# Three stretches of a hybrid decoder layer in another order: state-space outputs by kind, the attention projection's weights piece by piece, and the output projection's first weight splits among the mixed tiles

## The chip, the cores and the metric

The kernel runs on one core of a Trainium2 chip. The metric is the device time of one execution in microseconds (us). Engines are named as in the profile: PE is TensorE (PEld its weight loads), DVE VectorE, ACT ScalarE, POOL GpSimd, SP SyncE, which here only issues transfers. A q behind an engine's name (SPq) is its instruction queue.

## What is computed

One layer of a decoder trunk for 512 prompt tokens and 32 sample tokens (8 sequences of 4), all float32, model width 1024. Cut to what matters here:

```
h = x + 1/2 SwiGLU(RMSNorm(x));  n = RMSNorm(h);  P = n @ w_in
    [u | q | k | v | q_idx | k_idx | w_idx | gate_s5 | gate_att] = columns of P
S5  = GLU(GELU(y)),  s_t = A s_(t-1) + B u_t,  y = Re(C s_t) + D u_t   # 32 groups of 16 channels, 64 states
DSA = softmax attention over the top-k keys of an indexer, @ w_att_proj (512 x 1024)
h = h + (sigmoid(gate_s5) * S5 + sigmoid(gate_att) * DSA) @ w_out      # w_out 1024 x 1024
h = h + 1/2 SwiGLU(RMSNorm(h));  y = RMSNorm(h)
```

Outputs are y, the new keys, values and index keys, and the last states, for prompt and sample.

## The kernel before

Each engine runs an instruction stream written by hand; semaphores (`wait_ge`, `then_inc`) are all that ties them together. Nothing is scheduled by a planner, so the order in the code is the order on each engine. The 544 tokens are the moving columns of the large products, in two halves of 272 (`HALF`); weights are stationary in tiles of 128 x 128. The order is: first FFN, input projection, state-space part with the index scores, a loop of 32 steps for the prompt's attention, the sample's attention over the paged cache, attention projection, output projection, second FFN, final norm.

**State-space outputs** (PE, L833). `outputs(q4)` handles four pairs of groups; there are four calls, so 16 pairs in all. For one pair `gp` it writes columns `c0` to `c0+128` of two PSUM banks with three kinds of product: the lag kernels (`toep`, 128 rows by 72 columns of the array, L839), the carried states (`vst` against `yre` and `yim`, 64 rows by 64 columns, L842) and the sample's first states (`s0`, 64 rows by 8 columns, L847). The last two come in pairs, one on rows 0 to 63 and one on rows 64 to 127. The trace has two records for each float32 product. ACT copies the banks out (L1322), PE turns them (L855), and ACT applies GELU. ACT then issues eight transfers (L1349) that read a table of distance biases from DRAM into `biasmem`, where `yre` and `yim` lay. The sample's index scores follow on PE. POOL issues the first page of cached keys (L425) once these scores are done, and then waits for the bias table before it adds it to the masks (L1578) for the attention loop. In that loop PE's scores (L955) are taken over by DVE (L1893), and PE's next scores wait for that.

**Attention projection** (PE, L1083 to L1090). Before it the sample's values are gathered: eight steps of products with pages (L1065) run for each of two rounds, and each frees a page buffer and raises `kv_used` by one. `page_load` reuses four page buffers in turn. The weights `attw[0..3]` (512 KB each, L530, on SP's queue) lie where pages lay: `attw[0]` in pages of buffer 0, `attw[1]` and `attw[2]` in those of buffer 1, `attw[3]` in one of buffer 2. After the last page step PE turns the sample's result (L555 with `sg`, `rstd`), DVE copies it to `attT` (L1935), and the projection starts: eight tiles of two halves, each half four products over `attw`. Only the second half of the tokens holds sample columns.

**Mixed tiles and output projection.** For each of the eight tiles DVE multiplies the projection by the gate (`att_ev`), adds the state-space part (`mix_done`), ACT rounds the sum to a high part (`mix_high`, L1430, `acth`) and DVE takes the rest (`mix_low`, `actl`). The weights of the output projection are split in the same way: `high` on ACT (L1134, `w_high`), `low` on DVE (`w_low`). A `unit` (L568) is one output tile of the projection: eight blocks of three products (high by high, high by low, low by high) with two halves each, and it starts when `lo_done` counts the split of its weights and `att_ev` has all eight tiles; block k also waits for `mix_ready`. Line L1602 is a helper of DVE for all two-operand instructions.

Of the kernel before, what the change touches and what calls it, by code (L numbers as in the profile page):

```python
# [34 lines left out]
P = 128  # L35
D = 1024
DK = D // P
# [15 lines left out]
UC = NC + NB  # L53
# [49 lines left out]
def build(nc, t, out):  # L103

    ctx = ExitStack()
    with ctx:
# [33 lines left out]
        ps = ctx.enter_context(nc.psum_tensor("ps", [P, 8, 512], F32))  # L140
# [35 lines left out]
        toep = big[:, 0:4096].rearrange("p (g n) -> p g n", g=G)  # L176
# [5 lines left out]
        uch = uv[:, 0, 0:G * UC].rearrange("p (g c) -> p g c", g=G)  # L182
# [37 lines left out]
        def v(k):  # L220
# [65 lines left out]
        s = {n: sem(n) for n in (  # L286

            "gain_row_in", "par_in", "sample_const_in",
            "kidx_in", "bias_in", "att_w_in", "shift_out", "toep_in", "u_out", "u_in", "kidx_out", "kv_out", "res_out",

            "mm_done", "evac",

            "unit_done", "hi_done", "lo_done", "ffn_ev", "silu_done", "acth_done", "act_ready",

# [54 lines left out]
        FFN_UNITS = sum(2 * m + DK for _, m in GROUPS)  # L349
# [104 lines left out]
        def _(sp):  # L454
# [70 lines left out]
            first_pages(sp, 0)  # L525
            page_loads(sp, 0)

            sp.wait_ge(s["kv_used"], 4 + 31)
            for k in range(4):
                sp.dma_start(attw[k], t["w_att_proj"][0, P * k:P * k + P, :]).then_inc(s["att_w_in"], 16)  # L530

            sp.wait_ge(s["kv_used"], 4 + 32)
# [18 lines left out]
        def _(pe):  # L551
            def acc(dst, pairs, **kw):

                for k, (a, b) in enumerate(pairs):
                    ins = pe.matmul(dst, a, b, start=(k == 0), stop=(k == len(pairs) - 1), **kw)  # L555
                return ins
# [185 lines left out]
            for r in range(4):  # L742
                if r >= 2:
                    pe.wait_ge(s["lag_kernels_out"], r - 1)
                for q in range(4):
                    gp = 4 * r + q
                    for c, y in enumerate((yre, yim)):
                        for h in range(2):
                            sl = slice(64 * h, 64 * h + 64)
                            ins = pe.matmul(ps[0:16, 4 + 2 * (r % 2) + h, P * q:P * q + P], bbar[sl, c, gp, :], y[sl, gp, 0:CH, :],  # L750
                                            start=(c == 0), stop=(c == 1), skip_group_check=True)
# [50 lines left out]
            for q in range(4):  # L802
                for g4 in range(4):
                    gp = 4 * q + g4
# [27 lines left out]
            pe.wait_ge(s["scan_done"], 1)  # L832
            def outputs(q4):  # L833
                pair = ((2 * q4, slice(0, 64)), (2 * q4 + 1, slice(64, P)))
                for g2 in range(4):

                    gp, c0 = 4 * q4 + g2, P * g2
                    for o, (q, sl) in enumerate(pair):
                        pe.matmul(ps[0:UC, q, c0:c0 + P], uch[:, 2 * gp + o, :], toep[:, 2 * gp + o, :], start=True, stop=False, skip_group_check=True)  # L839
                    for c, y in enumerate((yre, yim)):  # L840
                        for q, sl in pair:
                            pe.matmul(ps[0:NC, q, c0:c0 + P], vst[sl, c, gp, 0:NC], y[sl, gp, 1:9, :].rearrange("p k i -> p (k i)"),  # L842
                                      start=False, stop=False, skip_group_check=True)

                    for c, y in enumerate((yre, yim)):
                        for q, sl in pair:
                            ins = pe.matmul(ps[NC:UC, q, c0 + 64:c0 + P], s0[sl, c, :, gp], y[sl, gp, 1:5, :].rearrange("p k i -> p (k i)"),  # L847
                                            start=False, stop=(c == 1), skip_group_check=True)
                ins.then_inc(s["chunk_outputs"], 1)
# [188 lines left out]
            for g in range(2):  # L1038
# [21 lines left out]
                for i in range(8):  # L1060
                    for half in range(2):
                        pe.wait_ge(kv_in[half][i % 4], 32 * (4 * g + 2 + i // 4 + 1))
                    for c in range(4):
                        q = slice(32 * c, 32 * c + 32)
# [3 lines left out]
                    if i == 7:  # L1068
                        for c in range(4):
                            q = slice(32 * c, 32 * c + 32)  # L1070
# [7 lines left out]
            for j in range(4):  # L1078
                ins = acc(ps[:, 6, 32 * j:32 * j + 32], [(osel[:, g, P * j:P * j + P], row_tok[:, g, :]) for g in range(2)])
            ins.then_inc(s["sample_att_turned"], 1)  # L1080
            pe.wait_ge(s["sample_att_out"], 1)


            pe.wait_ge(s["att_w_in"], 64)
            for i in range(DK):
                if i >= 2:
                    pe.wait_ge(s["att_ev"], i - 1)
                for h in range(2):
                    ins = acc(ps[:, 4 * (i % 2) + h, 0:HALF], [(attw[k][:, P * i:P * i + P], attT[:, k, h * HALF:(h + 1) * HALF]) for k in range(4)])
                ins.then_inc(s["att_mm"], 1)  # L1090

# [18 lines left out]
        def _(act_e):  # L1110
# [18 lines left out]
            def high(u, i, j):  # L1129

                act_e.wait_ge(raw_in[j], i * 16 + 16 * (u // 4 + 1))
                if not (isinstance(i, int) and u + 4 * i < 2):
                    act_e.wait_ge(s["unit_done"], i * 4 + (u - 1))
                act_e.activation(wh[:, j % 2, :, :], wraw[:, j, :, :], ACT.Copy).then_inc(s["hi_done"], 1)  # L1134
# [167 lines left out]
            for i in range(4):  # L1302
                n = first_tile["kv"] + i
                half, c0 = n % 2, 256 * (i % 2)
# [123 lines left out]
            def mix_high(i):  # L1428
                act_e.wait_ge(s["mix_done"], i + 1)
                act_e.activation(acth[:, i, :], fin_mix[:, i % 2, :], ACT.Copy).then_inc(s["mixh_done"], 1)  # L1430

            for i in range(DK - 1):
                mix_high(i)
            for j in range(2):
                high(FFN_UNITS + j, 0, j)
            mix_high(DK - 1)
            for j in range(DK - 1):
                high(FFN_UNITS + 2 + j, 0, (j + 2) % 4)
                scaled_high(j)
# [151 lines left out]
        def _(dve):  # L1591
# [38 lines left out]
            def low(u, i, j):  # L1630

                dve.wait_ge(s["hi_done"], i * 4 + (u + 1))
                tt(wl[:, j % 2, :, :], wraw[:, j, :, :], wh[:, j % 2, :, :].bitcast(F32), ALU.subtract).then_inc(s["lo_done"], 1)
# [308 lines left out]
            for i in range(DK):  # L1942
# [7 lines left out]
                tt(fin_mix[:, i % 2, :], mixed[:, i, :], sg[:, half, :], ALU.add).then_inc(s["mix_done"], 1)  # L1950
                if i:
                    mix_low(i - 1)
            for j in range(2):
                low(FFN_UNITS + j, 0, j)
            mix_low(DK - 1)
            for i in range(DK):
                dve.wait_ge(s["unit_done"], FFN_UNITS + i + 1)
# [46 lines left out]
```

## Time and profile before

| | us |
|---|---|
| median of 3 runs (lowest, highest) | 1542.78 (1541.96, 1546.97) |
| the profiled execution, its own time | 1543.36 |
| span of the profiled execution | 1541.7 |
| PE busy | 1456.2 (94%) |
| DVE busy / ACT busy / POOL busy | 608.9 / 452.9 / 262.1 |
| mean granted clock of TensorE | 0.974 of full |

The profiled execution took 1.7 us more than its span, and 0.6 us more than the median. TensorE's granted clock has two levels in the profile, 1.00 (2.4 GHz) and 0.50 (1.2 GHz). In a timeline each row is a run of equal instructions: start, length, engine, line, output and inputs, count, and in brackets how long the engine had been idle before and what ended that. Overlapping instructions of one row make its length less than the sum of their durations.

### The profile page before, as it was taken

What the parts mean: (1) busy time and instruction counts of PE and PEld (TensorE: products, weight loads), DVE (VectorE), ACT (ScalarE), POOL (GpSimd) and SP (SyncE); (2) the same over time, 40 slices, a digit from 0 to 9 for tenths busy, and PEclk for the clock granted to TensorE, in tenths of its full rate; (3) what the DMA queues carried; (4) which work ended last, traced back from release to release, by engine and by line L of the source; (5) the groups of instructions that cost most, each with busy time, mean ns of one, the idle gap of its engine ahead of it and who ended that gap; (6) DMA issues with size and microseconds to landing.
All of it is one profiled execution on the core that took longest, in us unless ns stands there. A gap on an engine that the chain in (4) does not pass through costs nothing. (4 is left out here: it accounts for less than half of the span.)

```text
span 1541.7 us, 27579 instructions
## 1 busy us (share of the span) xinstructions
PE 1456.2 (94%) x10734; PEld 1307.1 (85%) x10734; DVE 608.9 (39%) x957; ACT 452.9 (29%) x647; POOL 262.1 (17%) x458
## 2 busy tenths in 40 slices
PE   6999999999999989989999897979999999999996
PEld 5999999999967777657766684847999999999996
DVE  4333333434433377125555320204453343343344
ACT  4332222122320310145444322211342212221234
POOL 4000000685004049301133312110000000000000
PEclk9999999999999999989999998988999999999998
DMA  9532232332123452172111477752222323323221
GB/s 130 151 92 72 83 95 82 91 88 74 49 54 66 98 79 70 16 159 55 56 41 51 136 224 268 223 191 57 80 85 82 94 84 88 89 82 96 78 72 59
DMA packets 228747, 148.05 MB, mean 96 GB/s; under 512 B 29730, under 2 KB 211818, under 8 KB 228667
## 3 DMA queue, kind: packets, MB, share of 16 engines
q1 hardware_dynamic: 195904, 118.06, 26.2%
q0 software_dynamic: 7088, 19.65, 5.3%
q10 hardware_dynamic: 25674, 9.25, 3.6%
q8 instruction: 54, 0.88, 0.3%
q14 instruction: 27, 0.21, 0.1%
HBM read 139.62 MB, written 6.12 MB: 95 GB/s over the span
## 5 line engine op out<-in xcount | busy, mean ns | idle before, releaser
L1602 DVE TENSOR_TENSOR w_low<-wraw,w_high 128x1024 fp32r<-128x1024 f32 x144 | 180.1, 1252 | 318.3 <-ACT w_high L1134 318.3
L575 PE MATMUL ps<-hn_high,w_high 128*128 128x272 f32 x1408 | 292.3, 289 | 2.9 <-DVE w_low L1602 2.9
L575 PE MATMUL ps<-hn_high,w_low 128*128 128x272 f32 x1408 | 291.5, 288 | 0.0
L575 PE MATMUL ps<-hn_low,w_high 128*128 128x272 f32 x1408 | 291.2, 288 | 0.0
L1134 ACT ACTIVATE w_high<-wraw 128x1024 fp32r<-128x1024 f32 x144 | 152.4, 1060 | 447.8 <-PE ps L575 443.2
L575 PEld LDWEIGHTS ps<-hn_high,w_high 128*128 128x128 f32 x1408 | 221.8, 189 | 3.1 <-issue 3.0
L575 PEld LDWEIGHTS ps<-hn_low,w_high 128*128 128x128 f32 x1408 | 222.1, 189 | 0.0
L575 PEld LDWEIGHTS ps<-hn_high,w_low 128*128 128x128 f32 x1408 | 220.6, 189 | 0.0
L575 PE MATMUL ps<-act_high,w_high 128*128 128x272 f32 x832 | 174.3, 291 | 5.3 <-DVE w_low L1602 3.5
L575 PE MATMUL ps<-act_high,w_low 128*128 128x272 f32 x832 | 173.1, 290 | 0.0
L575 PE MATMUL ps<-act_low,w_high 128*128 128x272 f32 x832 | 172.7, 289 | 0.0
L575 PEld LDWEIGHTS ps<-act_high,w_high 128*128 128x128 f32 x832 | 131.6, 190 | 6.3 <-issue 3.9
L575 PEld LDWEIGHTS ps<-act_low,w_high 128*128 128x128 f32 x832 | 131.7, 190 | 0.0
L575 PEld LDWEIGHTS ps<-act_high,w_low 128*128 128x128 f32 x832 | 130.8, 190 | 0.0
L1493 POOL TENSOR_TENSOR kvtok<-qkT,apow 128x256 f32<-128x256 f32 x68 | 51.0, 781 | 260.6 <-DVEq L1786 252.7
L555 PE MATMUL ps<-wslot,hn 128*128 128x256 f32 (+3 forms) x416 | 85.0, 369 | 1.1 <-ACT uv L1299 1.1
L555 PEld LDWEIGHTS ps<-wslot,hn 128*128 128x128 f32 (+1 forms) x416 | 67.3, 181 | 18.6 <-issue 5.0
L555 PE MATMUL ps<-uv,wslot 128*128 128x272 f32 x256 | 68.5, 413 | 5.3 <-ACT sg L1373 5.3
L555 PEld LDWEIGHTS ps<-uv,wslot 128*128 128x128 f32 x256 | 48.0, 197 | 24.3 <-issue 15.9
L940 PE MATMUL ps<-hn,wslot 128*128 128x272 f32 x256 | 65.0, 399 | 0.0
L555 PE MATMUL ps<-hn,big 128*128 128x272 f32 x256 | 62.9, 399 | 1.0 <-ACT qkT L1399 0.5
L555 PE MATMUL ps<-hn,wslot 128*128 128x272 f32 (+1 forms) x272 | 61.2, 383 | 0.0
(328 smaller groups left out, 1637.3 us busy)
## 6 DMA issues: line engine op xcount, KB each, us to landing
wraw<-in_w_ffn_in SPq DMA_DIRECT2D x88, 512.0 KB, 3.9
wraw<-in_w_ffn_out SPq DMA_DIRECT2D x32, 512.0 KB, 3.9
wslot<-in_w_in SPq DMA_DIRECT2D x16, 512.0 KB, 3.9
wraw<-in_w_ffn_out SPq DMA_DIRECT2D x16, 384.0 KB, 3.4
wslot<-in_w_in SPq DMA_DIRECT2D x4, 1024.0 KB, 6.5
wslot<-in_cache_k POOLq DMA_DIRECT2D x16, 256.0 KB, 4.2
wslot<-in_w_s_glu SPq DMA_DIRECT2D x16, 256.0 KB, 3.1
wslot<-in_cache_k SPq DMA_DIRECT2D x16, 256.0 KB, 4.6
```

The lines of the kernel that those rows point to most:

```text
L555: ins = pe.matmul(dst, a, b, start=(k == 0), stop=(k == len(pairs) - 1), **kw)
L575: ins = pe.matmul(ps[:, bank + h, 0:HALF], a[:, w_at, k, :], x[:, lo_at(k) if x is x_lo else k, h * HALF:(h + 1) * HALF], start=(k == 0 an ...
L940: ins = pe.matmul(ps[:, 4 * slot + h, 0:HALF], slot_block(slot, k), hn[:, k, h * HALF:(h + 1) * HALF], start=(k == 0), stop=(k == DK - 1), ...
L1134: act_e.activation(wh[:, j % 2, :, :], wraw[:, j, :, :], ACT.Copy).then_inc(s["hi_done"], 1)
L1493: ins = pool.tensor_tensor(o, a, b, ALU.mult)
L1602: return dve.tensor_tensor(o, a, b, op)
```

## The change

- The output products of the state-space part are issued in order of their kind. For each four pairs all lag-kernel products come first, then all of the carried states, then all of the sample's states. `start`, which begins a new accumulation, is now set for the first product of each bank alone.
- Each of the four transfers of `attw` waits for the page step that frees its own buffer (29, 30, 30 and 31 instead of 31 for all).
- PE's wait for the sample's turned result moves from ahead of the projection to ahead of its second half.
- The first two splits of the output projection's weights move: on ACT to behind the mixed tiles 3 and 4, on DVE to behind tiles 5 and 6. Before, they stood between tile 6's and tile 7's rounding.

```diff
@@ SP
-            sp.wait_ge(s["kv_used"], 4 + 31)
             for k in range(4):
+                sp.wait_ge(s["kv_used"], 4 + (29, 30, 30, 31)[k])
                 sp.dma_start(attw[k], t["w_att_proj"][0, P * k:P * k + P, :]).then_inc(s["att_w_in"], 16)
@@ PE, outputs(q4)
-                for g2 in range(4):
-                    gp, c0 = 4 * q4 + g2, P * g2
+                quad = [(4 * q4 + g2, P * g2) for g2 in range(4)]
+                for gp, c0 in quad:
                     for o, (q, sl) in enumerate(pair):
-                        pe.matmul(ps[0:UC, q, c0:c0 + P], uch[...], toep[...], start=True, stop=False, skip_group_check=True)
+                        pe.matmul(ps[0:UC, q, c0:c0 + P], uch[...], toep[...], start=(c0 == 0), stop=False, skip_group_check=True)
+                for gp, c0 in quad:
                     for c, y in enumerate((yre, yim)):
...
+                for gp, c0 in quad:
                     for c, y in enumerate((yre, yim)):
...
@@ PE
-            pe.wait_ge(s["sample_att_out"], 1)
             pe.wait_ge(s["att_w_in"], 64)
...
                 for h in range(2):
+                    if i == 0 and h == 1:
+                        pe.wait_ge(s["sample_att_out"], 1)
@@ ACT
-            for i in range(DK - 1):
+            for i in range(DK):
                 mix_high(i)
-            for j in range(2):
-                high(FFN_UNITS + j, 0, j)
-            mix_high(DK - 1)
+                if i in (3, 4):
+                    high(FFN_UNITS + i - 3, 0, i - 3)
@@ DVE
                 if i:
                     mix_low(i - 1)
-            for j in range(2):
-                low(FFN_UNITS + j, 0, j)
+                if i in (5, 6):
+                    low(FFN_UNITS + i - 5, 0, i - 5)
             mix_low(DK - 1)
```

How the order changes on PE in the first call of `outputs` (`big` holds `toep`, `biasmem` holds `yre` and `yim`, `uv` the inputs and carried states, `s` is `s0`). Before:

```order
L839 MATMUL ps<-big,uv 72x128 x2
L842 MATMUL ps<-biasmem,uv 64x128 x4
L847 MATMUL ps<-biasmem,s 8x64 x4
L839 MATMUL ps<-big,uv 72x128 x2
L842 MATMUL ps<-biasmem,uv 64x128 x4
L847 MATMUL ps<-biasmem,s 8x64 x4
```

The change, two calls and the first turn:

```order
L838 MATMUL ps<-big,uv 72x128 x8
L842 MATMUL ps<-biasmem,uv 64x128 x16
L847 MATMUL ps<-biasmem,s 8x64 x16
L838 MATMUL ps<-big,uv 72x128 x8
L842 MATMUL ps<-biasmem,uv 64x128 x16
L847 MATMUL ps<-biasmem,s 8x64 x16
L855 MATMUL ps<-ident_sb,big 128x72 x8
```

The four repeats of three kinds in a call have become one; the products and their number are the same.

How the order changes on DVE at the last mixed tiles (`sg<-ps` is the multiplication by the gate, `biasmem<-big,sg` the sum, `act_low` the mixed tile's rest, `w_low` the weights' rest):

```order
+L1602 TENSOR_TENSOR w_low<-wraw,w_high 128x1024
 L1602 TENSOR_TENSOR sg<-ps,kvtok 128x544
 L1602 TENSOR_TENSOR biasmem<-big,sg 128x544
 L1602 TENSOR_TENSOR act_low<-biasmem,act_high 128x544
+L1602 TENSOR_TENSOR w_low<-wraw,w_high 128x1024
 L1602 TENSOR_TENSOR sg<-ps,idxm 128x544
 L1602 TENSOR_TENSOR biasmem<-big,sg 128x544
-L1602 TENSOR_TENSOR act_low<-biasmem,act_high 128x544
-L1602 TENSOR_TENSOR w_low<-wraw,w_high 128x1024 x2
-L1602 TENSOR_TENSOR act_low<-biasmem,act_high 128x544
+L1602 TENSOR_TENSOR act_low<-biasmem,act_high 128x544 x2
```

The two splits of weights stood behind the last tile's sum; they now stand ahead of the gate products of tiles 6 and 7.

## Rows read from the trace of the kernel before

**Rows 1.** Chain that ended last, 1031 to 1130 us: start, length, what

```profile
1031.99 6.43 DMA biasmem<-in_w_att_proj
1038.56 31.28 PE ps L555 x128
...
1073.36 57.05 PE ps L575 x432
```

**Rows 2.** Timeline, first call of outputs on PE: starts of the blocks

```profile
636.39 0.63 PE L839 MATMUL ps<-big,uv 128*72 128x128 f32 x4 [0.82 <-issue]
...
637.87 0.66 PE L839 MATMUL ps<-big,uv 128*72 128x128 f32 x4
...
642.37 0.66 PE L839 MATMUL ps<-big,uv 128*72 128x128 f32 x4
```

**Rows 3.** Timeline, 10 ns windows within one block: what runs then

```profile
636.64 0.38 PE L839 MATMUL ps<-big,uv 128*72 128x128 f32 x2
...
637.12 0.38 PE L842 MATMUL ps<-biasmem,uv 64*64 64x128 f32 x4
...
637.60 0.33 PE L847 MATMUL ps<-biasmem,s 64*8 64x64 f32 x6
```

**Rows 4.** Weight loads by line: duration in ns (min/median/max), first and last start

```profile
L839 PEld LDWEIGHTS ps<-big,uv x64: 139/143/145, 636.4 to 660.2; 128*72 128x72 f32 x64
...
L842 PEld LDWEIGHTS ps<-biasmem,uv x128: 128/133/134, 637.0 to 660.8; 64*64 64x64 f32 x128
...
L847 PEld LDWEIGHTS ps<-biasmem,s x128: 87/88/98, 637.5 to 661.2; 64*8 64x8 f32 x128
```

**Rows 5.** Timeline, start of the attention loop: POOL, DVE and PE

```profile
680.99 0.61 POOL L425 DMA_DIRECT2D wslot<-in_cache_k  x1 [50.60 <-issue]
...
684.03 0.86 POOL L1578 TENSOR_TENSOR uv<-biasmem,caus 128x128 f32<-128x128 f32 x2 [1.25 <-DMA biasmem<-scr_shift]
...
686.60 0.29 DVE L1893 CUSTOM_DVE_ANT_0 big<-ps,uv 128x128 f32<-128x128 f32 x1 [2.49 <-PE ps L955]
...
690.36 0.49 PE L955 MATMUL ps<-qkT 64*128 64x128 f32 x2
```

**Rows 6.** Issues of the bias table by line: first and last, us to landing

```profile
L1349 ACTq DMA_DIRECT2D biasmem<-scr_shift x8: 343/460/537, 664.1 to 667.5; - x8
...
DMA to landing us min/median/max: 6.3/11.6/16.4
```

**Rows 7.** Stretches: busy time of PE, PEld, DVE, ACT, POOL; PE clock, DMA share, GB/s

```profile
660.00:665.00 5.00, 3.63 (x42) 2.67 (x42) 0.00 (x0) 3.23 (x9) 0.00 (x0) 1.00 1.08 381
...
675.00:680.00 5.00, 4.40 (x81) 2.52 (x79) 0.69 (x1) 0.56 (x3) 0.00 (x0) 0.82 1.08 132
```

**Rows 8.** Timeline, end of the sample's attention: page steps, weights, turn, copy

```profile
1024.67 1.07 PE L1065 MATMUL ps<-biasmem,big 128*32 128x512 f32 x8
...
1029.53 1.06 PE L1065 MATMUL ps<-biasmem,big 128*32 128x512 f32 x8
...
1030.66 0.34 SPq L530 DMA_DIRECT2D wslot<-in_w_att_proj  x1
...
1033.34 1.97 PE L555 MATMUL ps<-rstd,sg 128*128 128x32 f32 x16 [0.89 <-DVE sg L1602]
1035.34 0.29 DVE L1935 COPY kvtok<-ps 128x128 f32<-128x128 f32 x1 [2.06 <-PE ps L555]
```

**Rows 9.** The four weight transfers of the attention projection by line

```profile
DMA to landing us min/median/max: 3.6/5.0/6.4
```

**Rows 10.** Timeline, last mixed tile and first output unit on DVE and PE

```profile
1069.87 0.72 DVE L1602 TENSOR_TENSOR sg<-ps,idxm 128x544 f32<-128x544 f32 x1 [1.55 <-PE ps L555]
...
1071.90 2.35 DVE L1602 TENSOR_TENSOR w_low<-wraw,w_high 128x1024 fp32r<-128x1024 f32 x2
...
1073.36 0.79 PE L575 MATMUL ps<-act_high,w_high 128*128 128x272 f32 x2 [3.53 <-DVE w_low L1602]
```

**Rows 11.** Stretches around the first output unit, columns as in rows 7

```profile
1073.30:1079.50 6.20, 6.14 (x27) 6.17 (x28) 1.59 (x2) 0.00 (x0) 0.00 (x0) 0.50 0.61 170
1079.60:1085.60 6.00, 6.00 (x49) 6.00 (x49) 2.64 (x3) 2.25 (x3) 0.00 (x0) 1.00 0.01 2
```

**Rows 12.** Timeline of PE in the attention loop: two idle times and what followed

```profile
802.64 3.55 PE L555 MATMUL ps<-uv,wslot 128*128 128x272 f32 x8 [1.27 <-ACT sg L1373]
...
816.94 2.07 PE L555 MATMUL ps<-uv,wslot 128*128 128x272 f32 x8 [1.06 <-ACT sg L1373]
```

More of the change, by code:

```diff
@@ L834, in outputs @@
                 pair = ((2 * q4, slice(0, 64)), (2 * q4 + 1, slice(64, P)))
-                for g2 in range(4):
-                    gp, c0 = 4 * q4 + g2, P * g2
+                quad = [(4 * q4 + g2, P * g2) for g2 in range(4)]
+                for gp, c0 in quad:
                     for o, (q, sl) in enumerate(pair):
-                        pe.matmul(ps[0:UC, q, c0:c0 + P], uch[:, 2 * gp + o, :], toep[:, 2 * gp + o, :], start=True, stop=False, skip_group_check=True)
+                        pe.matmul(ps[0:UC, q, c0:c0 + P], uch[:, 2 * gp + o, :], toep[:, 2 * gp + o, :], start=(c0 == 0), stop=False, skip_group_check=True)
+                for gp, c0 in quad:
                     for c, y in enumerate((yre, yim)):
```

## The prediction, made before the changed kernel ran

> **What bounds the kernel now.** I read the table of busy times first: PE works 94% of the span, so only what shortens PE's own work or its waits can move the end. The chain that ended last says where PE waits near its end: it goes through the transfer of the attention projection's weights into the 31.3 us of that projection, and from there into output projection and second FFN, one unbroken run of PE [rows 1]. Then the timelines of the three places that the change touches. At the state-space outputs PE never waits for another engine, so what counts there is the spacing of its own instructions [rows 2, 3]. At the other two it stands idle: 3.25 us for the weights, from the end of the turn at 1033.34 + 1.97 = 1035.31 to 1038.56 [rows 1, 8], and 3.53 us for the split of the output weights [rows 10]. What is saved at any of the three reaches the end if the next stretch only follows the last one; I go through that for each.
>
> **Outputs in order of kind.** A block of three kinds takes 637.87 - 636.39 = 1.48 us, or over four blocks (642.37 - 636.39)/4 = 1.50 us [rows 2]. Within a kind the spacing is tighter. Two running L839 records span 0.38 us and one lasts 0.27 us (L839's median is 273 ns), so they start 0.11 us apart. Two pairs of L842 also span 0.38 us at 0.27 each: 0.11 us for a pair. Three pairs of L847 span 0.33 us at 0.22 each: (0.33 - 0.22)/2 = 0.055 us [rows 3]. A block has four records of L839, four pairs of L842 and four of L847, since each product is two records: 4 x 0.11 + 4 x 0.11 + 4 x 0.055 = 1.10 us. The other 0.40 us is lost where the kind changes, three times in a block, 0.13 us each. The change leaves three such places in a call instead of twelve, so a call saves 3 x 0.40 = 1.2 us and the four calls **4.8 us**. From below: if the pause belongs to each new region of PSUM and not to the kind, 0. From above 6.4 us, if all of it went. I take 4.8, since two passes over one region within L842 show no pause [rows 3]. Behind it ACT's copies and the turns follow each call as before; ACT has far less than a call's time of work on each.
>
> What is late next is the bias table. POOL's first sum with it starts at 684.03, as the table's last transfer, issued at 667.5, lands after 16.4 us [rows 5, 6]. Today DVE takes the first scores at 686.60, so this costs nothing. PE needs DVE's first result only for its second scores at 690.36 [rows 5]; shifted by 4.8 us that is 685.56. If the table still landed where it does, POOL (0.45 us for one of its two sums) and DVE (0.29) would be through by 684.9, in time. But the transfers that land the table run with the 16 engines full, share 1.08 from 660 to 665 under the outputs of keys and values at 381 GB/s and 1.08 from 675 to 680 at 132 GB/s [rows 7]. An earlier issue then brings it forward little, and the two page transfers of POOL, now behind the table's end at 680.99 to 682.8, would move 4.8 us up and lie among them: 0.52 MB at 381 to 132 GB/s is 1.4 to 3.9 us, I take 2.3. The table then lands at 686.3, DVE is done at 687.1 and PE has lost **1.5 us**. If the table moves forward in full, the loss is 0. I take 0.8, the middle.
> The Trainium skill (DMA: Bandwidth & Descriptors, Queues, rings and completion order) says that each DMA engine goes round-robin between the queues that have work, so transfers from different queues share the same 16 engines. By that rule the loss is the full 1.5 us; the share of 1.08 under either queue speaks for it [rows 7], but no row shows the two large streams side by side.
>
> **Weights piece by piece, and the moved wait.** Today all four transfers are issued from 1030.66 on, the first landing after 3.6 us and the last after 6.4 [rows 8, 9], issued at 1031.99 and landing at 1038.4 [rows 1]. Now the first goes once page step 5 of 8 is through, before 1024.67; the second and third after the next step, 1024.67 + 1.07 = 1025.74. Only the fourth still waits for 1029.53 + 1.06, issued at 1030.66 with nothing ahead of it. That is the place of the first transfer today, so it lands after 3.6 us, at 1034.3. The turn of the sample's result ends at 1035.31, and this is then the later of the two: PE starts the projection at about 1035.35 instead of 1038.56, **3.2 us** earlier. If the fourth took 6.4 us, it would be 1037.1 and the gain 1.5 us. Ahead of these on SP's queue stand the last page loads, behind them the loads of the output weights, which are used 30 us later. The moved wait holds PE only ahead of the second half: DVE's copy ends at 1035.63, and the first half's eight records take longer than that. Left where it was, it would have cost the 0.4 us from 1035.31 to 1035.7, which is in the 3.2.
>
> **Splits among the mixed tiles.** PE's first unit starts at 1073.36, after DVE's first w_low [rows 10]. The gate product of tile 7 ends at 1069.87 + 0.72 = 1070.59, and with 0.2 us for the handoff PE can start at 1070.8: **2.5 us**. For that the splits must be hidden earlier. DVE is idle 1.55 us ahead of each tile's gate product and one split takes 2.35/2 = 1.2 us, so two tiles' idle times hold one each [rows 10]; 0.35 us is left. Without that cover each split would cost up to 1.2 us in the projection's rhythm. ACT has its high parts done a tile earlier. Late next are the last two mix_low, done by 1072.8; block 7 of the unit needs the last only some 5 us after its start.
> With the idle time goes its after-effect. From 1073.3 to 1079.5 PE ran at 0.50 of its clock, and at 1.00 afterwards [rows 11]: 6.2 us of work that takes 3.1 us at full clock, so **3.1 us** more if the clock holds. The idle time left is 1.0 us (1069.83 to 1070.8). In the attention loop 1.27 us of idling was followed by the same eight records in 3.55 us, 1.06 us by 2.07 us [rows 12]. 1.0 is on the side of the second, so I count it.
>
> **Sum.** 4.8 - 0.8 + 3.2 + 2.5 + 3.1 = 12.8 us. The profiled execution would go from 1543.4 to 1530.6 (its span from 1541.7 to 1528.9), and the median, which stands 0.6 lower, from 1542.8 to **1530.0**.
>
> **Rivals.**
> 1. The table takes its full price: loss 1.5 instead of 0.8, 1530.7. It differs from the forecast by less than a run can tell; the attention loop's start shows it.
> 2. The clock falls to half at the output projection all the same: 3.1 us not gained, 1533.1. For it: two idle times of 1.3 and 1.0 us in one kernel are not far apart, and where low and full clock lie depends on more than the gap. Against: rows 12.
> 3. The reorder does not do what it says, the pause belonging to each region: -4.8 + 0.8, 1534.0. Against it stands L842's even spacing on one region.
> 4. Slower: in long runs of one kind PE becomes bound by its weight loads, if they can't overlap in a longer run as they do over four. A load lasts 143, 133 and 88 ns [rows 4], while pairs start 0.11 and 0.055 us apart. At these durations end to end the outputs take 64 x 0.143 + 128 x 0.133 + 128 x 0.088 = 37.4 us and 12 pauses of 0.13 = 1.6, 39.0 in place of 16 x 1.50 = 24.0: 15.0 us more, and with the 8.8 gained elsewhere 1542.8 + 6.2 = 1549.0. The kernel is slower than before once the outputs pass 32.8 us. Against it: four pairs in a row already start without that price.
>
> **How the numbers follow.** Forecast with a table loss up to 1.0: 45%; rival 1: 25%; rival 2: 16%; rival 3: 6%; the fourth weight transfer or the splits missing their place, 1532 to 1535: 5%; slower: 2%; the rest 1%. Apart from that, wherever PE's work is moved against the low-clock stretches, one of them may be some 3.4 us longer or shorter in what it covers, as 1038.56 to 1042 is today, for 1.7 us either way; so the forecast's own range is 1527 to 1532.5. The range is **1526.5 to 1534.5**. Faster by more than 0.3% (4.6 us, about what a measurement of this kernel can tell from no change) is all but the last cases: 96%; within 0.3% 2%; slower 2%.
>
> **What would show it.** Outputs: the first L839 of the second call 4.8 us after that of the first (6.0 now), and the last products done 4.8 us earlier. Table: POOL's first L1578 at 684 or later, and PE idle before the second L955. Weights: no DMA ahead of the projection's L555, which starts right behind the turn. Splits: two single w_low between the tiles, PE idle about 1.0 us before L575, and the next 6 us at clock 1.00. It would be wrong if the kinds' pauses stay, if DVE's split delays the gate product of tile 6 or 7, or if new low-clock stretches appear in the loop.

## The result, and the profile after

| | before | changed kernel |
|---|---|---|
| median, us (lowest, highest; 5 runs each) | 1542.78 (1540.73, 1546.97) | 1530.23 (1526.55, 1534.53) |
| ratio, 95% interval | | 0.992 [0.9897, 0.9942] |
| profiled execution, its own time / span | 1543.36 / 1541.7 | 1526.55 / 1524.9 |
| mean granted clock of TensorE | 0.974 | 0.979 |
| PE busy, us | 1456.2 | 1445.4 |

The change takes 12.6 us off the median, where 12.8 was predicted (1530.0). The two profiled executions lie 16.8 us apart, so some 4 us of their difference aren't the change's; where they come from is said below.

**State-space outputs.** Timeline of PE in the changed kernel, first call of `outputs` and the start of the second; it answers to [rows 2, 3].

```profile
638.44 1.94 PE L838 MATMUL ps<-big,uv 128*72 128x128 f32 x16 [0.82 <-issue]
640.31 1.96 PE L842 MATMUL ps<-biasmem,uv 64*64 64x128 f32 x32
642.21 1.07 PE L847 MATMUL ps<-biasmem,s 64*8 64x64 f32 x32
643.21 0.98 PE L838 MATMUL ps<-big,uv 128*72 128x128 f32 x7
```

Each kind now has one row of all its records. The second call starts 643.21 - 638.44 = 4.77 us after the first; before, four blocks took 5.98. From the first product to the turn of the final states (L865) it is 660.40 - 638.44 = 21.96 us, and it was 663.20 - 636.39 = 26.81. The kinds keep their tight spacing over the longer rows: 16 pairs of L842 take 1.96 us, (1.96 - 0.27)/15 = 0.11 us a pair as before, though one weight load still lasts 133 ns. No bound by the weight loads has appeared.

**Start of the attention loop.** Timeline of the changed kernel, all engines; it answers to [rows 5].

```profile
681.83 0.46 PE L955 MATMUL ps<-qkT 64*128 64x128 f32 x2 [1.29 <-ACT biasmem L1362]
...
683.39 1.45 POOL L1578 TENSOR_TENSOR uv<-biasmem,caus 128x128 f32<-128x128 f32 x3 [4.88 <-DMA biasmem<-scr_shift]
684.00 0.29 DVE L1893 CUSTOM_DVE_ANT_0 big<-ps,uv 128x128 f32<-128x128 f32 x1 [4.17 <-POOL uv L1578]
...
686.08 0.48 PE L955 MATMUL ps<-qkT 64*128 64x128 f32 x2
```

POOL's wait for the table has grown from 1.25 to 4.88 us, and DVE's first scores now wait for POOL. But DVE is done at 684.29, 1.8 us before PE wants its second scores, and PE's row has no idle time. From the first scores to the second it is 4.25 us in either kernel: in this trace the table costs PE nothing.

**Attention projection.** Timeline of the changed kernel, PE and SP's queue; it answers to [rows 1, 8].

```profile
1015.03 0.34 SPq L530 DMA_DIRECT2D wslot<-in_w_att_proj  x1
1017.57 5.19 SPq L530 DMA_DIRECT2D biasmem<-in_w_att_proj  x3
```

```profile
1022.29 0.19 PEld L1065 LDWEIGHTS ps<-wslot,big 128*32 128x32 f32 x8 [0.83 <-DMA wslot<-in_cache_v]
1022.32 1.06 PE L1065 MATMUL ps<-wslot,big 128*32 128x512 f32 x8
...
1025.27 1.97 PE L555 MATMUL ps<-rstd,sg 128*128 128x32 f32 x16 [0.89 <-DVE sg L1602]
...
1027.08 0.99 PE L555 MATMUL ps<-kvtok,wslot 128*128 128x272 f32 x2
```

Three of the four transfers are issued before the last page step, and the projection starts 1027.08 - 1025.27 = 1.81 us after the turn's start; before it was 1038.56 - 1033.34 = 5.22. No DMA and no copy stands before it; the fourth transfer landed at 1026.77, 0.3 us ahead of this start. PEld's wait shows that the last page arrives late here: it landed at 1022.19, and the last two page steps span 2.09 us (1021.30 to 1023.39) where they take 1.92 in before and in the other traces. That is 0.17 us lost. The last page's transfer took 6.2 to 6.8 us in the nine traces with the early weights beside it and 5.3 to 5.6 in the four without; in the other eight of the nine it still landed over 0.7 us before its step.

**Output projection.** Timelines of DVE and of PE in the changed kernel; they answer to [rows 10].

```profile
1056.12 0.72 DVE L1602 TENSOR_TENSOR act_low<-biasmem,act_high 128x544 fp32r<-128x544 f32 x1
1056.75 1.22 DVE L1602 TENSOR_TENSOR w_low<-wraw,w_high 128x1024 fp32r<-128x1024 f32 x1
1058.38 0.72 DVE L1602 TENSOR_TENSOR sg<-ps,idxm 128x544 f32<-128x544 f32 x1 [0.41 <-PE ps L555]
```

```profile
1056.81 1.54 PE L555 MATMUL ps<-kvtok,biasmem 128*128 128x272 f32 x6
1059.55 0.49 PE L575 MATMUL ps<-act_high,w_high 128*128 128x272 f32 x2 [1.20 <-DVE sg L1602]
1059.87 0.41 PE L575 MATMUL ps<-act_low,w_high 128*128 128x272 f32 x2
```

DVE still idles 0.41 us ahead of the last gate product, so a split fits between two tiles (and where no low clock falls in the projection, it takes 29.58 us with the splits among its tiles as without them); PE waits 1.20 us for that product, no longer 3.53 for a split. Stretches of the changed kernel, columns as in [rows 7]; before, the first of them ran at clock 0.50 [rows 11]:

```profile
1059.50:1065.60 6.10, 6.05 (x48) 6.08 (x49) 1.73 (x3) 0.66 (x1) 0.00 (x0) 1.00 0.28 80
1065.60:1071.60 6.00, 6.00 (x50) 6.00 (x49) 2.65 (x3) 2.25 (x3) 0.00 (x0) 1.00 0.29 87
```

In this stretch the chain that ended last in the changed kernel has no weights and no split in it any more, only a page of cached values (for the fifth of the eight page steps; before has it too) and the last gate product (start, length, what):

```profile
1007.17 4.31 DMA wslot<-in_cache_v
...
1024.52 0.70 DVE sg L1602
...
1025.27 33.09 PE ps L555 x144
...
1058.38 0.74 DVE sg L1602
1059.12 0.43 issue
1059.55 40.49 PE ps L575 x322
```

**The span cut into stages** at PE's records, us. "Low" is the time in a stage at which the granted clock was at its lower level.

| stage | before | low | after | low | difference |
|---|---|---|---|---|---|
| start to first output product | 636.39 | 17.1 | 638.44 | 23.9 | +2.05 |
| state-space outputs, to L865 | 26.80 | 0 | 21.96 | 0 | -4.84 |
| to the first scores (L955) | 22.91 | 10.2 | 21.43 | 6.8 | -1.48 |
| first to second scores | 4.25 | 0 | 4.25 | 0 | 0 |
| attention loop | 186.58 | 9.0 | 184.66 | 3.8 | -1.92 |
| sample's attention over the pages | 156.40 | 18.3 | 154.53 | 16.7 | -1.87 |
| turn, to the projection's start | 5.23 | 3.4 | 1.81 | 0 | -3.42 |
| attention projection | 31.27 | 3.4 | 31.27 | 3.4 | 0 |
| idle before the first output unit | 3.53 | 0.6 | 1.20 | 0 | -2.33 |
| first output unit | 8.86 | 6.2 | 6.07 | 0 | -2.79 |
| rest | 459.46 | 11.6 | 459.25 | 9.4 | -0.21 |

The four stages that the change meant to shorten give 4.84 + 3.42 + 2.33 + 2.79 = 13.4 us. The other differences come to -3.4 us and belong to stages in which PE's own code is the same.

### The profile page after: what moved, and what is told of

Same layout as the page of the kernel before. It is cut to its first block and busy times, and to the rows that moved or that the text cites. A ratio compares the mean times of both kernels' runs of the same rounds, so it can differ in the third digit from the quotient of the medians.

```text
span 1524.9 us, 27578 instructions
## 1 busy us (share of the span) xinstructions
PE 1445.4 (95%) x10734; PEld 1302.3 (85%) x10734; DVE 609.1 (40%) x957; ACT 452.8 (30%) x647; POOL 264.1 (17%) x458
```

## The experiments

**Each part alone.** Three kernels have one part of the change each: the new order in `outputs`; the four waits of the weights and the moved wait of PE; the splits' new places. Each edit is the respective part of the diff shown above and nothing else.

> The kernel before with the outputs in order of their kind and nothing else. My theory: the four calls take 4.8 us less, the bias table lands about where it did but still before PE's second scores need it, so the whole saving reaches the end: ratio 0.9969 of the kernel before (-4.8 us), within 2 us for where the low-clock stretches fall. If the table takes its full price, PE idles 1.5 us before its second scores and the saving is 3.3 us. If the saving belongs to less low clock and not to the pauses, the outputs stretch itself is not shorter than 26.8 us from the first product to the last states' turn.

> The kernel before with the four weight transfers of the attention projection each waiting for its own buffer and the moved wait, nothing else. My theory: PE's wait of 3.25 us ahead of the projection goes, the projection follows the turn directly: -3.2 to -3.4 us. Rival: the earlier transfers share the DMA engines with the last page loads and hold up page steps 6 to 8; then a new idle time of up to 1.3 us stands before L1065 and the gain is 2 us.

> The kernel before with the two weight splits among the mixed tiles, nothing else. My theory: the idle time before the first output unit falls from 3.5 to 1.2 us (-2.3) and the low clock behind it goes (-2.8 to -3.1): -5.1 to -5.4 us. Rival: the low clock has to do with where the stretch falls and not with the idle time; then the first unit still takes 9 us instead of 6.0 and the gain is 2.3 us.

| kernel | median (lowest, highest; runs) | ratio, 95% |
|---|---|---|
| outputs_only | 1539.79 (1535.63, 1543.82; 11) | 0.9983 [0.9968, 0.9998] |
| weights_only | 1537.96 (1535.44, 1541.15; 11) | 0.9972 [0.9960, 0.9983] |
| splits_only | 1536.86 (1533.97, 1545.14; 12) | 0.9972 [0.9957, 0.9988] |
| before, beside them | 1542.3 (28 runs) | |

The stages of these kernels' traces (us) show each part acting in its own stage alone:

| | outputs | turn to projection | projection (low) | idle before unit | first unit |
|---|---|---|---|---|---|
| before | 26.80 | 5.23 | 31.27 (3.4) | 3.53 | 8.86 |
| outputs_only | 21.95 | 5.39 | 31.25 (3.4) | 3.53 | 8.87 |
| weights_only | 26.80 | 1.81 | 29.58 (0) | 3.53 | 8.69 |
| splits_only | 26.80 | 5.00 | 32.08 (5.1) | 1.20 | 6.08 |
| changed kernel | 21.96 | 1.81 | 31.27 (3.4) | 1.20 | 6.07 |

Weights: 1.81 in place of 5.23 is 3.4 us; the median moved by 4.3. Part of the rest may be the clock. In all four traces in which PE waits for the weights, the clock is low in the projection for 3.4 to 5.1 us, and it takes 31.25 to 32.08 us. In the nine without that wait, five have no low clock there and take 29.58 us, and four (the changed kernel's first trace among them) have 3.3 to 3.4 us of it and take 31.20 to 31.29. So low clock followed the wait each time and came without it only sometimes: an after-effect of about 1.7 us in some executions, which the prediction had not counted. The mean granted clock over all timed executions is higher too: 0.9761 with the weights' part and 0.9760 with the splits', against 0.9742 for before beside them, with standard errors of 0.0004 to 0.0007. Splits: 2.33 + 2.78 = 5.1 us in the trace, 5.4 by the medians, 4.3 by the ratio. Outputs: 4.85 us in the trace, but only 2.6 by the ratio, with 4.9 at the interval's edge. That called for a second measurement.

**Outputs again, and the whole change again.** The outputs' part and the whole change were timed once more.

> The kernel before with the outputs in order of their kind, timed once more, since the first time gave 2.5 us less with an interval of 0.3 to 4.9. My theory: its trace takes 21.95 us for the outputs again and PE's second scores wait for nothing, so both timings together come near 4.8 us less. Rival: something later gives 2 us back in the usual execution, then the second timing stays near 2.5 us less too.

> The changed kernel once more, beside its parts. My theory: the parts add up, -4.8 -3.3 -5.2 = -13.3 us, ratio 0.9914; what the first profile of it showed beyond that (16.8 us) is low clock that fell otherwise and should average out. Rival: the parts help each other and the whole is over 2 us more than their sum.

outputs_only_again measured 1538.25 (1531.95 to 1540.96, 12 runs) beside 1542.1 (16 runs), ratio 0.9975 [0.9963, 0.9987], and its stage again 21.95 us. after_again measured 1529.08 (1525.37 to 1531.22, 5 runs), ratio 0.9909 [0.9891, 0.9927]; the whole was measured a third time beside a later experiment (after_third, 1529.42, 0.9918 [0.9895, 0.9941]).

> The changed kernel beside the one above, for the difference of the two on one chip: 1.1 us by my theory, which the times may not resolve, as single executions of either spread over 6 us; the traces should.

So the outputs' part is worth 2.6 and 3.9 us by its two ratios, with intervals that reach to 4.9 and 5.7: neither the 4.8 of the theory nor the 2.5 of its rival. The stage gives 4.85 in every trace with the new order alone (and 21.94 to 21.96 in the whole change's); whether a part of it is given back on average later is not settled. One sign of it is the mean granted clock of the timed executions, 0.9737 against 0.9742 for before beside them and 0.9742 against 0.9755 the second time. Since 0.001 of it is about 1.5 us of 1540, low clock that falls elsewhere could be 1 to 2 us; the standard errors of 0.0004 to 0.0006 leave it open.

The expectation that PE's second scores wait for nothing did not hold in outputs_only_again. Timeline of this kernel, POOL and PE:

```profile
680.14 1.44 POOL L1578 TENSOR_TENSOR uv<-biasmem,caus 128x128 f32<-128x128 f32 x3 [6.70 <-DMA biasmem<-scr_shift]
...
681.10 0.29 PEld L955 LDWEIGHTS ps<-qkT 64*128 64x128 f32 x2 [0.44 <-DVE tiny L1893]
```

Here the way from the outputs to the first scores had 3.4 us of low clock in place of 6.8, so PE was there 0.9 us sooner (20.53 us for 21.43). The table came 0.9 us later (23.9 us after the first L865 for 23.0). PE then waited for DVE, and DVE for POOL's sum with the table: 4.34 us from the first to the second scores in place of 4.25. The table is thus the next bound. It costs about 0.1 us here, and half of the changed kernel's slack of 1.8 us was there only because of the low clock before it. The parts' ratios sum to 2.6 + 4.3 + 4.3 = 11.2 us, or 12.5 with the second one for the outputs, the whole is worth 12.3 to 14.0 by its three ratios: within the intervals the parts add up, and none needs another.

**Is it the change of kind that costs?** In the outputs, the carried states (64 x 64) and the sample's states (64 x 8), which use the same 64 rows of the array, are done pair by pair again, while the lag kernels stay together.

```diff
                 for gp, c0 in quad:
                     for c, y in enumerate((yre, yim)):
...
-                for gp, c0 in quad:
                     for c, y in enumerate((yre, yim)):
```

> The changed kernel, but in each call the carried states and the sample's states of a pair of groups stay together, four times 4+4 products, behind all lag-kernel products. Both use 64 rows of the array; they differ in their columns (64 against 8). My theory: each change between them costs a pause as any change of kind, nine pauses a call instead of three, so the stretch of the outputs is 24 x 0.13 = 3.1 us longer than the changed kernel's 21.95: 25.1 us. Rival: only the change of rows (128 to 64) costs; then the stretch stays within 0.5 us of 22.

Timeline of PE in this kernel, its first call of `outputs`:

```profile
639.99 1.94 PE L838 MATMUL ps<-big,uv 128*72 128x128 f32 x16 [0.82 <-issue]
641.86 0.65 PE L842 MATMUL ps<-biasmem,uv 64*64 64x128 f32 x8
642.44 0.40 PE L846 MATMUL ps<-biasmem,s 64*8 64x64 f32 x8
642.77 0.66 PE L842 MATMUL ps<-biasmem,uv 64*64 64x128 f32 x8
643.35 0.40 PE L846 MATMUL ps<-biasmem,s 64*8 64x64 f32 x8
...
645.51 1.75 PE L838 MATMUL ps<-big,uv 128*72 128x128 f32 x14
```

The same products now need 25.00 us, 3.04 more than in the changed kernel. In a call, carried and sample's states alternate in eight rows; with the lag kernels' row that makes nine rows, each ended by a change of kind (the last by the next call's or the turn's products), against three in the changed kernel. That is six more in each of four calls: 3.04 / 24 = 0.127 us for each. That is the 0.13 us of the prediction, and it is paid although the rows stay the same and only the columns go from 64 to 8. A pause for each new region of PSUM is ruled out, since a region is still opened only once here, and since the long rows of one kind pass from region to region without it. At 0.127 us the 36 changes that the new order saves give 4.6 of the 4.84 us; the other 0.3 is not attributed (the changes to and from the lag kernels may cost more, or the fewer `start` flags may save some). The two kinds also differ in the PSUM partitions that they write and in their moving columns (128 and 64), so the run shows what a change of kind costs, not which property of the kind makes it. The one execution took 1531.2 us.

The Trainium skill (TensorEngine Tiling (Array Packing), Key Properties) says that changing the tiling mode drains the engine. The 0.127 us agree with a drain of that kind; the page has no price, and no run here shows what the engine does in the pause.

**What does the bias table wait for?** Two kernels take away what lies beside the table on the 16 DMA engines. In the first, the outputs of keys and values wait until the table is there (the final states' outputs, which stood behind them, go ahead; the diff is cut to the lines that matter).

```diff
+            sp.wait_ge(s["bias_in"], 16 * HEADS)
             sp.wait_ge(s["evac"], EV0 + first_tile["gs"])
             for a, n in ((ktok, "k"), (vtok, "v")):
                 sp.dma_start(out[n + "_prompt"][0, 0]...).then_inc(s["kv_out"], 16)
```

> The changed kernel with SP's transfers of the prompt's keys and values (2.2 MB) behind the landing of the bias table. My theory, that the DMA engines are full and shared between the queues: the table, issued from the same point of ACT's stream, lands 5 us earlier against the end of the outputs than in the changed kernel, and POOL's first sum no longer waits for it; the loop starts no earlier, since PE's second scores never waited for the table. Rival, that the table's transfers are bound by themselves: they land where they did, within 1 us.

In the second, POOL issues its two pages only behind its wait for the table.

```diff
-            first_pages(pool, 2)
             pool.wait_ge(s["bias_in"], 16 * HEADS)
+            first_pages(pool, 2)
```

> The changed kernel with POOL's first two page transfers behind the landing of the bias table instead of ahead. By the shared engines the table lands 1.4 to 2.3 us earlier than in the changed kernel against the end of the outputs. Rival: the pages slip in beside the table at no price, under 0.5 us. The time of the kernel stays the same in either.

They took 1528.81 and 1531.16 us in one execution each, which tells nothing at a scatter of some 6 us; the traces tell more. The table's issues and landings by line, in the changed kernel and then with the outputs of keys and values behind it (durations in ns, starts in us):

```profile
L1350 ACTq DMA_DIRECT2D biasmem<-scr_shift x8: 342/756/1611, 661.3 to 668.4; - x8
...
DMA to landing us min/median/max: 7.4/11.8/14.9
```

```profile
L1351 ACTq DMA_DIRECT2D biasmem<-scr_shift x8: 343/478/509, 659.0 to 662.4; - x8
...
DMA to landing us min/median/max: 5.8/10.6/15.8
```

Measured from the first L865, after which the table is issued, POOL's first sum with it starts after 684.03 - 663.20 = 20.8 us in before, 683.39 - 660.40 = 23.0 in the changed kernel (23.2 with the outputs' part alone, 681.95 - 658.77), 678.25 - 658.05 = 20.2 without the outputs of keys and values beside it. With the pages behind it, the last landing comes at 21.0 (issued at 670.4, 12.8 us on its way, L865 at 662.28). One kernel's traces differ in this by up to 2 us: POOL's first sum comes after 19.8 to 21.8 us in the three traces with the old order of the outputs and after 22.2 to 23.9 in the eight with the new one and nothing moved beside the table.

So of the 4.85 us by which the first of the eight transfers came forward, 2.2 are lost again. Most of that is due to the outputs of keys and values. Their place didn't move (the first is issued 20.7 us after the first product in the changed kernel, 20.8 in before), so the table moved into them. They cost it 2.8 us, where 5 were expected, and POOL still waited 1.98 us for the table. A part of this shows already in the issues: the last of the eight starts 8.0 us after L865 in the changed kernel, 4.3 in before and 4.35 without these outputs. So it came forward by only 1.1 us of the 4.85. The kernel with the pages behind the table fits the 1.4 to 2.3 us expected, but its fourth landing is already 1.2 us earlier, at 14.5 for 15.6, before the changed kernel issues its pages at 16.3. From the fourth landing to the eighth it takes 6.5 us for 7.3 (7.2 to 8.5 in the other traces of the new order): the pages cost some 0.8 us, not 2.

Neither is worth moving. PE's two first scores are 4.25 us apart in the changed kernel, 4.41 and 4.33 in these two. The 4.41 holds no wait but slower first products (a row of 0.62 us for 0.46). The 4.33 does hold a wait for DVE, since with the pages behind the table POOL issues them at the wrong time:

```profile
684.83 0.61 POOL L425 DMA_DIRECT2D wslot<-in_cache_k  x1 [50.54 <-issue]
686.05 0.56 POOL L425 DMA_DIRECT2D wslot<-in_cache_k  x1 [0.61 <-issue]
686.63 1.46 POOL L1578 TENSOR_TENSOR uv<-biasmem,caus 128x128 f32<-128x128 f32 x3
```

The Trainium skill (DMA: Bandwidth & Descriptors, Queues, rings and completion order) has each DMA engine go round-robin between the queues that have work. By that rule a transfer that meets another on the way takes longer, and the traces agree in kind: 2.2 us of 4.85 lost, and 2.8 regained without the outputs of keys and values. They don't show that all is lost, which was my upper bound, and the longer issues on ACT's queue are not in that rule.

**What is the moved wait worth?** The changed kernel with PE's wait for the sample's turned result back in its old place.

```diff
+            pe.wait_ge(s["sample_att_out"], 1)
             pe.wait_ge(s["att_w_in"], 64)
...
-                    if i == 0 and h == 1:
-                        pe.wait_ge(s["sample_att_out"], 1)
```

> The changed kernel with PE's wait for the sample's turned result back ahead of the projection. My theory: the projection starts 0.4 us later behind the turn, 2.2 us after the turn's start instead of 1.8, and nothing else moves. Rival: it costs nothing, since the fourth weight transfer is the one that is late; then still 1.8.

Timeline of this kernel, DVE and PE:

```profile
1032.98 0.29 DVE L1934 COPY kvtok<-ps 128x128 f32<-128x128 f32 x1 [2.06 <-PE ps L555]
1033.32 0.30 PEld L555 LDWEIGHTS ps<-kvtok,wslot 128*128 128x128 f32 x2 [0.49 <-DVE kvtok L1934]
1033.33 0.73 PE L555 MATMUL ps<-kvtok,wslot 128*128 128x272 f32 x2 [0.38 <-DVE kvtok L1934]
```

The turn stage takes 2.36 us, not 1.81 (2.2 was expected): the wait is worth 0.55 us, where 0.4 was in the prediction. The idle row is 0.38; the rest is that the projection no longer overlaps the turn's last products. In one execution (1532.73 us) this can't be seen; the stage shows it.

**Can the last 1.2 us go too?** The first unit needs all of the projection only to free PSUM for it, so it can start one gate product sooner, with the wait for the last one ahead of the second unit.

```diff
-            pe.wait_ge(s["att_ev"], DK)
+            pe.wait_ge(s["att_ev"], DK - 1)
             with pe.Fori(0, 2) as i:
                 for j in range(4):
+                    if j == 1:
+                        pe.wait_ge(s["att_ev"], DK)
```

> The changed kernel, with PE starting the first output unit once tile 6's gate product has freed its banks, and waiting for tile 7's only ahead of the second unit. My theory: the idle time of 1.2 us before the unit goes (to under 0.1), the last blocks of the unit find their mixed tiles ready (the last is done 2.5 us after the projection's end, PE asks for it after 5 us), so the time is 1.1 to 1.2 us less than the changed kernel's. Rival: the unit runs into the mixed tiles 6 and 7 and waits inside, and the gain is under 0.3 us.

Timeline of PE in this kernel:

```profile
1057.61 0.62 PE L555 MATMUL ps<-kvtok,biasmem 128*128 128x272 f32 x2
1057.87 0.62 PE L575 MATMUL ps<-act_high,w_high 128*128 128x272 f32 x2
1058.32 0.41 PE L575 MATMUL ps<-act_low,w_high 128*128 128x272 f32 x2
```

The idle time is gone, and the unit overlaps the projection's last products. It measured 1529.99 us (1525.69 to 1532.26, 6 runs), ratio 0.9919 [0.9900, 0.9938], beside 1529.42 and 0.9918 for the changed kernel in the same comparison. In the trace the step from the projection's end to the end of the first unit on PE is 1.4 us shorter (5.85 for 7.27), where 1.1 to 1.2 were expected; in the medians no gain shows, and one of this size can't be resolved. I don't call it an improvement.

**Why single executions differ by 6 us.** The thirteen traces have the same code in the sample's attention in all but its last step, yet that stage takes 154.5 to 160.5 us. Two numbers of each trace account for it: how long PE waited for pages there, and how long the granted clock was low. Waits of PE by what it waited for (us in total, times, longest), first the changed kernel and then the kernel with the outputs' part alone:

```profile
PE ps L1065 <- DMA wslot<-in_cache_v: 5.8, 2, 3.0
```

```profile
PE ps L1065 <- DMA wslot<-in_cache_v: 7.7, 2, 4.3
```

| | stage | waits for pages | low clock | stage - waits - low/2 |
|---|---|---|---|---|
| changed kernel | 154.53 | 5.8 | 16.7 | 140.4 |
| before | 156.40 | 7.0 | 18.3 | 140.3 |
| after_again | 156.81 | 7.1 | 20.0 | 139.7 |
| outputs_only | 157.98 | 7.7 | 20.0 | 140.3 |
| pages_behind_table | 158.06 | 9.4 | 17.5 | 139.9 |
| kv_out_behind_table | 160.53 | 9.4 | 23.5 | 139.4 |

Half of the low time is about what work loses in it (the 0.25 and 0.45 us for two products, further down, make it 0.44; with that the thirteen lie between 140.7 and 141.5). What remains is 139.4 to 140.7 us in all thirteen. With the part of the loop and of the way to it (183.4 to 186.6 and 20.5 to 22.9 us, again with more low clock in the longer ones) this covers what the profiled execution of the changed kernel was better than its gain. The stage from the start to the outputs (634.3 to 640.3 us) does not follow its low clock (17 to 31 us); what moves it stays open.

## Why the prediction was right

- **The bound.** PE's own chain was the right one to read: each of the three places gave the end what it saved in its stage, and for the whole change nothing behind them took it back that a comparison can resolve (for the outputs alone it is open).
- **Outputs, 4.8 us:** 4.84 in the trace, for the reason given: 0.127 us for a change of kind, measured by putting 24 of them back; that covers 4.6 of it. Rival 3 (the pause belongs to a region, 1534.0) and rival 4 (bound by weight loads, 1549.0) are refuted by the rows above. The median of this part alone stays open between 2.6 and 4.8.
- **Bias table, 0.8 us lost:** mis-sized; it is 0 in the changed kernel's traces and 0.1 in outputs_only_again. The mechanism is there, the size was wrong in two places. I had the table held back in full by the outputs of keys and values and the pages on top of that, landing at 686.3 in before's time. It came forward by (684.03 - 636.39) - (683.39 - 638.44) = 2.7 of the 4.85 us. The slack before PE's second scores covered the rest. The two pages, sized at 2.3 us, cost some 0.8. Rival 1 (the full 1.5) did not occur.
- **Weights, 3.2 us:** 3.42. The fourth transfer was in time, though it took 4.3 us and not 3.6 in this trace, and PE's own turn set the start. The difference is the moved wait, 0.55 for 0.4, since the projection overlaps the turn's last products and doesn't start behind their end. Two effects were not in the sum: the last page's step, 0.17 us later in the first trace, and the low clock behind the wait for the weights, about 1.7 us, which that trace did not shed.
- **Gap, 2.5 us:** 2.33. The idle time left is 1.20, where I had 1.0: from the gate product's end on DVE to PE it takes 0.43 us, as the chain shows, where I had put 0.2.
- **Low clock behind it, 3.1 us:** 2.79, the first unit 6.07 in place of 8.86. I had halved the 6.2 us at the low clock. The kernel with the weights' part alone has both speeds in one unit (timeline of PE):

```profile
1068.20 0.66 PE L575 MATMUL ps<-act_high,w_low 128*128 128x272 f32 x2
1068.65 0.66 PE L575 MATMUL ps<-act_high,w_high 128*128 128x272 f32 x2
...
1074.35 0.41 PE L575 MATMUL ps<-act_high,w_high 128*128 128x272 f32 x2
1074.60 0.41 PE L575 MATMUL ps<-act_low,w_high 128*128 128x272 f32 x2
```

  Two products start 0.45 us after the last two at clock 0.50 and 0.25 us at 1.00: a factor of 1.8, not 2. So 6.2 us hold work for 3.4, and 2.8 are won. Rival 2 (the clock falls all the same) did not occur in any of nine traces with a gap of 1.2 us or none, while in all four with a gap of 3.5 us the clock was low behind it or from just before it. How much of the unit it covers varies: 6.2, 6.2 and 5.8 us in three of the four, 2.9 in outputs_only_again, where the unit took 7.40 us. There the low clock costs 1.3 us and not 2.8.
- **The sum:** -4.84 + 0 - 3.42 - 2.33 - 2.79 = -13.4 us in the traces, 12.8 predicted, 12.6 measured by the medians. Table and gaps erred in opposite directions, and the prediction left out the clock behind the weights' wait, so the agreement within 0.2 us is in part luck: the changed kernel's three medians alone spread over 1.2 us.

## What to carry to other kernels

- On PE count the changes of kind in a run of small matrix products, not the products: each change of rows or columns of the weights cost 0.13 us here, as much as a pair of products, and sorting by kind is free where the accumulation allows it. A stall of PE should be priced with the clock behind it: 3.5 us of idling cost 6.3 with what followed (4.9 in one of four traces), and bringing it to 1.2 us gave back 5.1. A transfer that is issued earlier lands earlier only by what its neighbours on the DMA engines leave it, here 2.7 of 4.85 us; what decides is the slack of the engine that wants it, and that slack differs between executions with the low clock before it.

## What the runs showed of the hardware

- A pause of 0.127 us also where the products before and after use the same 64 rows and only 8 columns in place of 64. Whether it would go if the sample's products were widened to 64 columns wasn't tried. Between products on rows 0 to 63 and on rows 64 to 127 of one kind there is no such pause: 16 pairs in 1.96 us.
- ACT's queue took 342 to 1611 ns for one issue of the table, median 756, while the outputs of keys and values were under way; without them it was 343 to 509, median 478, and before 343 to 537, median 460 [rows 6]. The eight issues ran until 668.9. ACT's next work (L1357) started at 669.50, when PE's product was there, so some 0.6 us more of this would have held ACT up.
- Stretches of the changed kernel at that time, columns as in [rows 7], after the 381 and 132 GB/s of before:

```profile
660.00:665.00 5.00, 2.93 (x20) 2.11 (x20) 0.98 (x3) 4.72 (x8) 0.00 (x0) 0.71 1.07 335
665.00:670.00 5.00, 4.46 (x80) 3.43 (x78) 1.38 (x2) 2.63 (x4) 0.00 (x0) 0.60 1.05 287
670.00:675.00 5.00, 4.14 (x82) 2.62 (x82) 0.69 (x1) 0.80 (x4) 0.00 (x0) 1.00 1.05 262
675.00:680.00 5.00, 3.60 (x16) 1.46 (x12) 1.31 (x2) 1.30 (x5) 1.17 (x2) 1.00 1.12 160
```

The share is full in all four while the rate falls from 335 to 160 GB/s: the two streams now mix (the last output of keys and values lands at 678.0), and a full share does not tell how many bytes move.
